# An attention, experts and delta-net stack: output products without waits in the merge, lower halves moved from GpSimd to VectorE, and fewer products in the stick-breaking sums

## Chip, cores and metric

One Trainium2 chip, one core of it. The metric is the device time of one execution in microseconds; lower is better. All data is float32. Products that must be exact to nearly 24 bits are made of three TensorE products of rounded halves (below).

## What is computed

The reference is two blocks on 512 tokens of width 1024. Only the parts that the change touches are shown.

```python
def rms_norm(x, g):                      # rmsnorm is the same
    return x * rsqrt(mean(x * x, -1) + EPS) * g

def first_block(x, ...):
    h = rms_norm(x, norm_attn)
    ...                                  # two attentions: o_mla, o_dil
    gates = sigmoid(gate_pre.reshape(B, S, 2, D) + b_gate)
    merged = gates[:, :, 0] * (o_mla @ w_o_mla) + gates[:, :, 1] * (o_dil @ w_o_dil)
    x = x + merged @ w_out               # the merge
    h2 = rms_norm(x, norm_ffn)
    return x + hier_moe(h2, ...)         # 32 experts, two for each token

def second_block(x, ...):                # layer 0: attention, layer 1: delta net
    for layer in range(2):
        h = rmsnorm(x, norm_mix_g[layer]) * (1.0 + scale_m) + shift_m
        x = x + gate_m * mixed(h)
        h = rmsnorm(x, norm_ffn_g[layer]) * (1.0 + scale_f) + shift_f
        x = x + gate_f * swiglu(h, ffn_w_in[layer], ffn_w_out[layer])
    return rmsnorm(x, final_norm_g)
```

Half of the heads of layer 0's attention are "stick" heads (stick-breaking attention): with z the scores and l = log(1 + exp(z)), the weight of key s for query t (s < t) is exp(z[s,t] - sum of l[r,t] over r from s to t-1). So each weight needs a sum of l over the keys from s on.

## The kernel before

Everything lies transposed: features or keys on the 128 partitions, the 512 tokens on the free axis. `xT` is the residual in 8 tiles of 128 x 512 (`KD` = 8). Five engines run programs of their own, in an order written out by hand, and meet at semaphores; `k.meet()` between stages makes every compute engine wait for the last work of the others.

**Split products.** A weight tile of 128 x 1024 (a unit) is loaded by DMA on SP's queue, its upper half is a rounded copy by ACT (`split_hi_act`, L338), its lower half is the difference, by DVE (`split_lo_dve`, L344) or by POOL (`split_lo_pool`, L353). `split_product_pe` (L463 to L465) then does, for each of 8 rows kk, three products of 512 columns: hi x hi, lo x hi, hi x lo. `low_mark` says which semaphore tells PE that a unit's lower half is there; `pool_units` is how many units POOL does. `load_weights_sp` loads a unit into one of four slots once the slot's former lower half has been taken. The ring of upper and lower halves has 3 places in the merge and 4 in the SwiGLU: `split_hi_act` for unit i waits for the product that is that many units back.

**Merge.** For j = 0 to 7 and both branches n, PE makes a gate product (a split product) and a plain product (L1562) into banks 4*(j%2) to 4*(j%2)+3. ACT takes the sigmoid, DVE multiplies (L1604, counted as `evacuated`), adds the two branches (L1607), makes lower halves of the units 2j+3 and 2j+4, and at last takes the lower half of the merged row j (L1611, counted as `merged`). Then follow 8 output products (units 16 to 23) into the banks 0 to 3: the first waits for `merged` 8, the ones for j = 1, 2, 3 wait for the addition of the product before (`added`, L1542), the later ones for the addition four products back.

**Norms.** While the last products run, ACT squares each row of x and POOL adds the squares up (`fold_pool`, L508); DVE makes the last addition (L515) and the stage ends in a meeting. Then PE sums over partitions (L519), ACT takes the root (L525; before it stands a load of ACT's table, ACT_TABLE_LOAD, since other functions were in use), DVE takes the reciprocal (L543), and for each of the 8 rows DVE multiplies (L550), ACT rounds (L535) and DVE takes the lower half (L559); PE's next products take the rows in turn. `norm` (before the experts and at the end) has no lower halves. `block_norm` (before layer 0's attention) and `split_norm` (before both SwiGLUs and the delta net) have weights converted beside them: two blocks by POOL, or unit 0 by DVE and units 1 to 3 by POOL. `first_norm` is another function.

**Stick.** For each of 8 heads, PE makes scores for key tiles j = 0 to 3 over the queries from j*128 on (512, 384, 256, 128 columns; L2505). DVE makes -|z| (L2576, L2578), ACT takes Exp and Ln (L2548, L2552; two table loads a head), DVE adds max(z, 0) and masks the first 128 columns (L2583, L2586), which gives l. For head h-1, PE then makes for each key tile i the score again (L2515), the mask (L2517), and minus the sums of l: `neg_from` times tile i's l and `neg_ones` times each later tile's (L2519, 4+3+2+1 products); ACT takes Exp (L2558) and copies into the same scratch. For head h-2, PE multiplies with the values (L2529) and DVE copies the result (L2590). All these products are float32 and show as two instructions each. The fourth tile of head h-1 goes into the bank that the first one had, so it waits for ACT's Exp of the first.

## Time and profile before

| what | value |
|---|---|
| median of 3 runs | 2894.82 us (2888.44 to 2900.26) |
| the profiled execution: its time, its span | 2895.99 us, 2894.7 us |
| busy share of the span: PE, DVE, ACT, POOL | 89%, 47%, 31%, 16% |
| mean granted TensorE clock | 0.934 of full |

Start times in rows of the trace count from the start of the span. The profiled execution ended 1.3 us after its span and was 1.2 us above the median of the runs. "Idle before" tells how long an engine stood still ahead of a group and what ended that.

### The profile page before, as it was taken

Reading aid. Unit: us, or ns where it says so; the run is one execution under the profiler, and the core shown is the slowest. Engines: PE = TensorE matmul, PEld = TensorE weight load, DVE = VectorE, ACT = ScalarE, POOL = GpSimd, SP = SyncE. Lnnn points to the kernel's source line nnn. Section 1 sums busy time; section 2 is a strip of 40 time slices with the busy share of each in tenths; the row PEclk is TensorE's granted clock in tenths of the full one; section 3 lists DMA queues with packets and bytes.
Section 4 is the critical chain, followed back from the end, with each engine's and each line's share of the span. In section 5 each row is a group of like instructions: output and inputs, shape, how many; then the busy total and the mean of one; then the engine's idle time right before and its main releaser. Section 6 shows DMA issues by size and latency. Waiting matters only on the chain.

```text
span 2894.7 us, 33686 instructions
## 1 busy us (share of the span) xinstructions
PE 2590.6 (89%) x13305; PEld 2049.3 (71%) x13305; DVE 1363.5 (47%) x2290; ACT 895.6 (31%) x1610; POOL 456.6 (16%) x449
## 2 busy tenths in 40 slices
PE   6999989998699994998988999979889899899997
PEld 4798987665455552876676878767787776687876
DVE  7886745322311114426537666345645644433333
ACT  4344435321211111325533212233322322332222
POOL 4563422000122222200011000010200200200001
PEclk9899988998799996998998999989989899899999
DMA  5453311132389994320014566232002002232322
GB/s 185 138 153 96 116 59 45 52 87 73 146 337 415 417 405 148 94 73 1 1 59 145 182 194 185 73 80 59 1 13 75 1 18 77 71 98 77 113 79 67
DMA packets 315084, 340.86 MB, mean 118 GB/s; under 512 B 18800, under 2 KB 271856, under 8 KB 302512
## 3 DMA queue, kind: packets, MB, share of 16 engines
q1 hardware_dynamic: 292720, 281.79, 29.7%
q0 software_dynamic: 22208, 56.93, 5.7%
q8 instruction: 106, 1.74, 0.3%
q14 instruction: 50, 0.41, 0.0%
HBM read 372.21 MB, written 16.78 MB: 134 GB/s over the span
## 4 chain that ended last, share of the span: by engine, by line
PE 72%; DVE 6%; ACT 4%; DMA 4%; issue 1%; ACTq 0%; POOL 0%; DVEq 0%; POOLq 0%
PE bank L463 13%; PE bank L465 13%; PE bank L464 13%; PE bank L2926 4%; PE bank L2166 4%; DMA sb_expert_weights<-w_up 3%; PE bank L2192 2%; PE bank L1562 2%; PE bank L399 2%; PE bank L401 2%; PE bank L400 2%; PE bank L669 1%; PE bank L689 1%; PE bank L679 1%; DVE sb_scratch L543 1%
## 5 line engine op out<-in xcount | busy, mean ns | idle before, releaser
L344 DVE TENSOR_TENSOR sb_w_lo<-sb_weights,sb_w_hi 128x1024 fp32r<-128x1024 f32 (+2 forms) x215 | 239.9, 1125 | 508.3 <-ACT sb_w_hi L338 508.0
L463 PE MATMUL bank<-sb_h_hi,sb_w_hi 128*128 128x512 f32 x1040 | 420.9, 405 | 7.1 <-DVE sb_w_lo L344 7.1
L465 PE MATMUL bank<-sb_h_hi,sb_w_lo 128*128 128x512 f32 x1040 | 408.3, 393 | 0.0
L464 PE MATMUL bank<-sb_h_lo,sb_w_hi 128*128 128x512 f32 x1040 | 407.7, 392 | 0.0
L338 ACT CAST sb_w_hi<-sb_weights 128x1024 fp32r<-128x1024 f32 x224 | 215.5, 969 | 555.2 <-PE bank L465 488.4
L508 POOL TENSOR_TENSOR sb_scratch<-sb_scratch 128x512 f32<-128x512 f32 x30 | 38.7, 1292 | 1309.3 <-ACT sb_scratch L498 1309.3
L463 PEld LDWEIGHTS bank<-sb_h_hi,sb_w_hi 128*128 128x128 f32 x1040 | 197.0, 189 | 61.6 <-issue 21.7
L464 PEld LDWEIGHTS bank<-sb_h_lo,sb_w_hi 128*128 128x128 f32 x1040 | 197.1, 189 | 45.7 <-issue 5.3
L399 PE MATMUL bank<-sb_wide,sb_h_hi 128*128 128x512 f32 (+2 forms) x512 | 206.4, 403 | 23.8 <-DVE sb_h_lo L556 8.6
L465 PEld LDWEIGHTS bank<-sb_h_hi,sb_w_lo 128*128 128x128 f32 x1040 | 196.4, 189 | 43.0
L400 PE MATMUL bank<-sb_wide,sb_h_hi 128*128 128x512 f32 (+2 forms) x512 | 199.2, 389 | 0.0
L401 PE MATMUL bank<-sb_wide,sb_h_lo 128*128 128x512 f32 (+2 forms) x512 | 199.0, 389 | 0.0
L463 PE MATMUL bank<-sb_hidden_hi,sb_w_hi 128*128 128x512 f32 x352 | 138.7, 394 | 12.9 <-DVE sb_hidden_lo L1772 12.9
L399 PEld LDWEIGHTS bank<-sb_wide,sb_h_hi 128*128 128x128 f32 x512 | 122.0, 238 | 37.8 <-issue 22.7
L465 PE MATMUL bank<-sb_hidden_hi,sb_w_lo 128*128 128x512 f32 x352 | 137.8, 391 | 0.0
L464 PE MATMUL bank<-sb_hidden_lo,sb_w_hi 128*128 128x512 f32 x352 | 137.7, 391 | 0.0
L381 DVE TENSOR_TENSOR sb_wide<-sb_weights,sb_wide 128x1024 fp32r<-128x1024 f32 (+2 forms) x62 | 88.2, 1427 | 98.3 <-ACT sb_wide L374 98.2
L2166 PE MATMUL bank<-sb_expert_weights,sb_moe 128*64 128x256 f32 x960 | 124.4, 385 | 9.4 <-DMA sb_expert_weights<-w_up 7.3
L401 PEld LDWEIGHTS bank<-sb_wide,sb_h_lo 128*128 128x128 f32 x512 | 122.1, 238 | 10.3
L400 PEld LDWEIGHTS bank<-sb_wide,sb_h_hi 128*128 128x128 f32 x512 | 122.6, 240 | 9.2
L374 ACT CAST sb_wide<-sb_weights 128x1024 fp32r<-128x1024 f32 (+2 forms) x72 | 72.0, 1003 | 167.7 <-PE bank L401 139.6
L2166 PEld LDWEIGHTS bank<-sb_expert_weights,sb_moe 128*64 128x64 f32 x960 | 77.7, 138 | 44.6 <-issue 13.6
(512 smaller groups left out, 4799.7 us busy)
## 6 DMA issues: line engine op xcount, KB each, us to landing
sb_weights<-ffn_w_in SPq DMA_DIRECT2D x88, 512.0 KB
sb_weights<-w_in SPq DMA_DIRECT2D x52, 512.0 KB
sb_xT<-ada_w POOLq DMA_DIRECT2D x24, 1024.0 KB, 6.8
sb_weights<-ada_w SPq DMA_DIRECT2D x24, 1024.0 KB
sb_expert_weights<-w_down SPq DMA_DIRECT2D x22, 1024.0 KB, 9.8
sb_expert_weights<-w_gate SPq DMA_DIRECT2D x20, 1024.0 KB, 12.6
sb_expert_weights<-w_up SPq DMA_DIRECT2D x19, 1024.0 KB, 15.2
sb_weights<-ffn_w_out SPq DMA_DIRECT2D x32, 512.0 KB
```

The costliest lines, as they stand in the source:

```text
L338: act.copy(u.hi[:, 0:u.kt, :], u.chunk.w).then_inc(*k.hi.one())
L344: dve.tensor_tensor(u.lo[:, 0:u.kt, :], u.chunk.w, u.hi[:, 0:u.kt, :].bitcast(F32), ALU.subtract).then_inc(*k.lo.one())
L374: act.copy(b.hi, b.chunk.w).then_inc(*k.block_hi.one())
L381: dve.tensor_tensor(b.lo, b.chunk.w, b.hi.bitcast(F32), ALU.subtract).then_inc(*k.block_lo.one())
L399: pe.matmul(out, hi[:, r, tokens], b.hi[:, kk, :], start=r == 0, stop=False)
L400: pe.matmul(out, hi[:, r, tokens], b.lo[:, kk, :], start=False, stop=False)
L401: return pe.matmul(out, lo[:, r, tokens], b.hi[:, kk, :], start=False, stop=last)
L463: pe.matmul(bank[:], u.hi[:, kk, :], act[0][:, kk, :], start=first and kk == 0, stop=False)
L464: pe.matmul(bank[:], u.hi[:, kk, :], act[1][:, kk, :], start=False, stop=False)
L465: mm = pe.matmul(bank[:], u.lo[:, kk, :], act[0][:, kk, :], start=False, stop=last and kk == u.kt - 1)
L2166: mm = pe.matmul(halves(bank, n)[:, 0:FF], r.xbT[p % 2][:, at:at + CAP], loads[n].w[:, kk, :], start=kk == 0, stop=kk == KD - 1)
L2926: mm = pe.matmul(bank[:, hh * P:(hh + 1) * P], left(hh), right(hh), start=True, stop=True)
```

## The change

The merge's first output product waits for the evacuation of the banks that it writes, and then row by row for the merged rows; the next three wait for no addition. In the norms ACT runs a Sqrt of one column into a new tile `early` before anything else. `block_norm`'s block 0 gets its lower half from DVE. `split_norm` leaves only unit 1 to POOL; DVE does unit 2 within the last rows of the norm and unit 3 after them. In the stick, the key tiles go in the order 3, 2, 1, 0; DVE adds the next tile's l into the tiles 2 and 1 (behind their first 128 columns, before the mask), so that PE needs only `neg_from` times tile i and one more product with tile i+1, whose matrix is `neg_before` or, for i = 0, `neg_ones`.

```diff
--- before.py
+++ after.py
@@ -79,7 +79,7 @@
         "chunk_all": chunk,
         "neg_from": -(part >= col).astype(np.float32),
         "neg_ones": -np.ones((P, P)),
-        "sb_keep": part < col,
+        "neg_before": -(part < col).astype(np.float32),
         "sb_mask": np.where(part < col, 0.0, NEG),
         "causal": np.where(col <= part, 0.0, NEG),
         "levels": np.concatenate(levels, 1),
@@ -519,6 +519,11 @@
     k.nc.tensor.matmul(k.bank[3][:], k.const("ones"), k.scr[10][:], start=True, stop=True).then_inc(*k.h_sum.one())
 
 
+def root_table_act(k):
+
+    k.nc.scalar.activation(k.early[:], k.eps[:], ACT.Sqrt).then_inc(*k.act_step.one())
+
+
 def norm_root_act(k, ready):
     act = k.nc.scalar
     act.wait_ge(*ready)
@@ -536,7 +541,7 @@
                            ).then_inc(*k.h_hi.one())
 
 
-def norm_rows_dve(k, gain, shift, split):
+def norm_rows_dve(k, gain, shift, split, late=None):
     dve = k.nc.vector
     inv = k.scr[4]
     dve.wait_ge(*k.h_root.at(1))
@@ -549,6 +554,8 @@
             h = k.scr[5 + kk % 4][:] if split else k.hT[:, kk, :]
             dve.scalar_tensor_tensor(out=h, in0=k.xT[:, kk, :], scalar=gain(kk), in1=inv[:], op0=ALU.mult,
                                      op1=ALU.mult).then_inc(*k.h_rows.one())
+        if late and kk == KD - 1:
+            split_lo_dve(k, late)
         if split and kk > 0:
             j = kk - 1
             dve.wait_ge(*k.h_hi.at(j + 1))
@@ -564,6 +571,7 @@
 def norm(k, gain):
 
     norm_sum_pe(k)
+    root_table_act(k)
     norm_root_act(k, k.h_sum.at(1))
     norm_rows_dve(k, gain, None, None)
 
@@ -571,8 +579,9 @@
 def block_norm(k, gain, shift, blocks):
 
     norm_sum_pe(k)
+    root_table_act(k)
     block_hi_act(k, blocks[0])
-    block_lo_pool(k, blocks[0])
+    block_lo_dve(k, blocks[0])
     norm_root_act(k, k.h_sum.at(1))
     block_hi_act(k, blocks[1])
     block_lo_pool(k, blocks[1])
@@ -582,16 +591,18 @@
 
 def split_norm(k, gain, shift, split, units):
 
-    k.pool_units = 3
+    k.pool_units = 1
     norm_sum_pe(k)
+    root_table_act(k)
     split_hi_act(k, units[0])
     norm_root_act(k, k.h_sum.at(1))
     for u in units[1:4]:
         split_hi_act(k, u)
-        split_lo_pool(k, u)
+    split_lo_pool(k, units[1])
     norm_shift_act(k, shift, split)
     split_lo_dve(k, units[0])
-    norm_rows_dve(k, gain, shift, split)
+    norm_rows_dve(k, gain, shift, split, units[2])
+    split_lo_dve(k, units[3])
 
 
 
@@ -944,7 +955,7 @@
     k.consts = k.sb("consts", [P, k.at_["dist0"][0]])
     k.rows = k.sb("rows", [P, sum(n for _, n in ROWS.values())])
     k.pos = k.sb("pos", [P, 2 * NT], I32)
-    k.eps, k.kgain = k.sb("eps", [P, 1]), k.sb("kgain", [P, 1])
+    k.eps, k.kgain, k.early = k.sb("eps", [P, 1]), k.sb("kgain", [P, 1]), k.sb("early", [P, 1])
     k.posf = k.sb("posf", [P, 2 * NT])
     k.cos1, k.sin1 = k.sb("cos1", [P, NT, ROPE // 2]), k.sb("sin1", [P, NT, ROPE // 2])
     k.cos2, k.sin2 = k.sb("cos2", [P, NT, ROPE2 // 2]), k.sb("sin2", [P, NT, ROPE2 // 2])
@@ -1563,11 +1574,11 @@
             mm.then_inc(*k.projected.one())
             ch.freed = [k.projected.last()]
     for j in range(KD):
-        if j < 4:
-            pe.wait_ge(*k.merged.at(KD) if j == 0 else k.added.at(j))
-        else:
+        if j == 0:
+            pe.wait_ge(*k.evacuated.at(2 * (KD - 1)))
+        elif j >= 4:
             pe.wait_ge(*k.added.at(j - 3))
-        split_product_pe(k, units[2 * KD + j], merged, k.bank[j % 4])
+        split_product_pe(k, units[2 * KD + j], merged, k.bank[j % 4], rows=None if j else k.merged)
 
 
 def merge_act(k, units, merged):
@@ -2490,6 +2501,9 @@
     pool.tensor_copy(padded[HD:P, 3:H:2, :], q[HD:P, 1:4, :]).then_inc(*k.padded_pool.one())
 
 
+STICK = (3, 2, 1, 0)
+
+
 def stick_pe(k, padded, kb, vb, o):
     pe = k.nc.tensor
     for s in range(H + 2):
@@ -2499,9 +2513,9 @@
             pe.wait_ge(*k.padded_act.at(h // 2 + 1))
             pe.wait_ge(*k.padded_dve.at(2))
         if h < H:
-            for j in range(NT):
+            for j in STICK:
                 if h >= 1:
-                    pe.wait_ge(*k.reduced.at(4 * (h - 1) + j + 1))
+                    pe.wait_ge(*k.reduced.at(4 * h - j))
                 pe.matmul(k.bank[j][:, 0:S - j * P], kb[:, h // 2, j * P:(j + 1) * P], padded[:, h, j * P:S],
                           start=True, stop=True).then_inc(*k.scored.one())
         h = s - 1
@@ -2515,9 +2529,11 @@
                 pe.matmul(bank[:, 0:n], kb[:, h // 2, i * P:(i + 1) * P], padded[:, h, i * P:S],
                           start=True, stop=False)
                 pe.matmul(bank[:, 0:P], k.const("ident"), k.const("sb_mask"), start=False, stop=False)
-                for j in range(i, NT):
-                    mm = pe.matmul(bank[:, (j - i) * P:n], k.const("neg_from" if j == i else "neg_ones"),
-                                   k.scr[4 * (h % 3) + j][:, 0:S - j * P], start=False, stop=j == NT - 1)
+                mm = pe.matmul(bank[:, 0:n], k.const("neg_from"), k.scr[4 * (h % 3) + i][:, 0:n], start=False,
+                               stop=i == NT - 1)
+                if i < NT - 1:
+                    mm = pe.matmul(bank[:, P:n], k.const("neg_before" if i else "neg_ones"),
+                                   k.scr[4 * (h % 3) + i + 1][:, 0:n - P], start=False, stop=True)
                 mm.then_inc(*k.turned.one())
         h = s - 2
         if 0 <= h < H:
@@ -2542,13 +2558,13 @@
     for s in range(H + 1):
         h = s
         if h < H:
-            for j in range(NT):
+            for j in STICK:
                 n, u = S - j * P, k.scr[4 * (h % 3) + j]
-                act.wait_ge(*k.maxed.at(4 * h + j + 1))
+                act.wait_ge(*k.maxed.at(4 * h + NT - j))
                 act.activation(u[:, 0:n], u[:, 0:n], ACT.Exp).then_inc(*k.exped.one())
-            for j in range(NT):
+            for j in STICK:
                 n, u = S - j * P, k.scr[4 * (h % 3) + j]
-                act.wait_ge(*k.exped.at(4 * h + j + 1))
+                act.wait_ge(*k.exped.at(4 * h + NT - j))
                 act.activation(u[:, 0:n], u[:, 0:n], ACT.Ln, bias=1.0).then_inc(*k.rooted.one())
         h = s - 1
         if h >= 0:
@@ -2568,22 +2584,27 @@
     for s in range(H + 2):
         h = s
         if h < H:
-            for j in range(NT):
+            for j in STICK:
                 n, u, z = S - j * P, k.scr[4 * (h % 3) + j], k.bank[j]
-                dve.wait_ge(*k.scored.at(4 * h + j + 1))
+                dve.wait_ge(*k.scored.at(4 * h + NT - j))
                 if h >= 3:
                     dve.wait_ge(*k.weighed.at(h - 2))
                 dve.tensor_scalar(u[:, 0:n], z[:, 0:n], 0.0, None, ALU.max).then_inc(*k.dve_step.one())
                 dve.wait_ge(*k.dve_step.last())
                 dve.scalar_tensor_tensor(out=u[:, 0:n], in0=u[:, 0:n], scalar=-2.0, in1=z[:, 0:n], op0=ALU.mult,
                                          op1=ALU.add).then_inc(*k.maxed.one())
-            for j in range(NT):
+            for j in STICK:
                 n, u, z = S - j * P, k.scr[4 * (h % 3) + j], k.bank[j]
-                dve.wait_ge(*k.rooted.at(4 * h + j + 1))
+                dve.wait_ge(*k.rooted.at(4 * h + NT - j))
                 dve.scalar_tensor_tensor(out=u[:, 0:n], in0=z[:, 0:n], scalar=0.0, in1=u[:, 0:n], op0=ALU.max,
                                          op1=ALU.add).then_inc(*k.dve_step.one())
                 dve.wait_ge(*k.dve_step.last())
-                dve.tensor_tensor(u[:, 0:P], u[:, 0:P], k.const("sb_keep"), ALU.mult).then_inc(*k.reduced.one())
+                if j in (1, 2):
+                    dve.wait_ge(*k.reduced.last())
+                    dve.tensor_tensor(u[:, P:n], u[:, P:n], k.scr[4 * (h % 3) + j + 1][:, 0:n - P], ALU.add
+                                      ).then_inc(*k.dve_step.one())
+                    dve.wait_ge(*k.dve_step.last())
+                dve.tensor_tensor(u[:, 0:P], u[:, 0:P], k.const("before"), ALU.mult).then_inc(*k.reduced.one())
         h = s - 2
         if 0 <= h < H:
             dve.wait_ge(*k.weighed.at(h + 1))
```

## Rows read from the trace of the kernel before

**Rows 1.** The page's chain that ended last: shares of the span by engine.
```profile
PE 72%; DVE 6%; ACT 4%; DMA 4%; issue 1%; ACTq 0%; POOL 0%; DVEq 0%; POOLq 0%
```

**Rows 2.** Waits of PE from 681 to 748 us: total, times, longest.
```profile
PE bank L463 <- DVE sb_xT L1542: 9.2, 3, 3.0
...
PE bank L463 <- DVE sb_merged_lo L1611: 4.5, 1, 4.5
```

**Rows 3.** Timeline of DVE at the end of the merge's gates: start, duration.
```profile
663.89 0.69 DVE L1604 TENSOR_TENSOR sb_scratch<-sb_scratch,bank 128x512 f32<-128x512 f32 x1 [8.21 <-PE bank L1562]
...
685.29 0.68 DVE L1611 TENSOR_TENSOR sb_merged_lo<-sb_scratch,sb_merged_hi 128x512 fp32r<-128x512 f32 x1
```

**Rows 4.** Windows of the merge: PE, PEld, DVE, ACT, POOL busy, clock, DMA, GB/s.
```profile
681.60:686.03 4.43, 0.00 (x0) 0.00 (x0) 4.25 (x5) 0.62 (x1) 0.00 (x0) 0.84 0.74 207
...
686.03:694.30 8.27, 8.22 (x24) 6.29 (x24) 0.00 (x0) 0.00 (x0) 0.00 (x0) 0.68 0.59 143
...
697.30:704.70 7.40, 7.37 (x24) 5.55 (x24) 0.00 (x0) 0.61 (x1) 0.00 (x0) 0.77 0.24 71
...
730.90:747.20 16.30, 16.30 (x73) 13.17 (x71) 3.21 (x4) 2.95 (x4) 3.87 (x3) 1.00 0.00 0
```

**Rows 5.** The last window before the experts' products.
```profile
780.00:803.00 23.00, 10.82 (x52) 10.05 (x52) 10.74 (x64) 0.20 (x1) 2.92 (x3) 0.50 0.09 24
```

**Rows 6.** Timeline of the norm before the first SwiGLU, all engines.
```profile
1523.78 1.04 ACT L338 CAST sb_w_hi<-sb_weights 128x1024 fp32r<-128x1024 f32 x1 [1.19 <-DVE sb_scratch L515]
...
1524.84 1.28 ACT L525 ACT_TABLE_LOAD   x1
...
1524.96 1.23 DVE L344 TENSOR_TENSOR sb_w_lo<-sb_weights,sb_w_hi 128x1024 fp32r<-128x1024 f32 x1 [1.64 <-ACT sb_w_hi L338]
...
1526.86 3.35 DVE L543 RECIPROCAL sb_scratch<-sb_scratch 128x512 f32<-128x512 f32 x1 [0.68 <-ACT sb_scratch L525]
...
1527.93 7.41 POOL L353 TENSOR_TENSOR sb_w_lo<-sb_weights,sb_w_hi 128x1024 fp32r<-128x1024 f32 x3 [9.40 <-ACT sb_w_hi L338]
...
1530.25 5.63 DVE L550 SCALAR_TENSOR_TENSOR sb_scratch<-sb_xT,sb_mod,sb_scratch 128x512 f32<-128x512 f32 x2
...
1536.59 0.80 PE L449 MATMUL bank<-sb_h_hi,sb_w_hi 128*128 128x512 f32 x1 [10.79 <-DVE sb_h_lo L559]
...
1543.76 1.62 DVE L559 SCALAR_TENSOR_TENSOR sb_h_lo<-sb_scratch,sb_mod,sb_h_hi 128x512 fp32r<-128x512 f32 x2
```

**Rows 7.** Instructions of line L550: minimum, median, maximum in ns.
```profile
L550 DVE SCALAR_TENSOR_TENSOR sb_scratch<-sb_xT,sb_mod,sb_scratch x32: 739/743/2881, 1156.5 to 2515.3; 128x512 f32<-128x512 f32 x32
```

**Rows 8.** Timeline of the norm before layer 0's attention.
```profile
1153.15 3.35 DVE L543 RECIPROCAL sb_scratch<-sb_scratch 128x512 f32<-128x512 f32 x1 [3.73 <-ACT sb_scratch L525]
...
1158.98 0.77 PE L399 MATMUL bank<-sb_wide,sb_h_hi 128*128 128x512 f32 x1 [6.68 <-DVE sb_h_lo L559]
```

**Rows 9.** Timeline of ACT: the table loads of the two plain norms.
```profile
752.17 1.28 ACT L525 ACT_TABLE_LOAD   x1 [3.55 <-PE bank L519]
...
2881.45 1.28 ACT L525 ACT_TABLE_LOAD   x1 [2.18 <-PE bank L519]
```

**Rows 10.** Window of the first pair of products after the SwiGLU's norm.
```profile
1541.10:1549.30 8.20, 8.20 (x37) 6.83 (x36) 4.15 (x7) 2.18 (x3) 0.00 (x0) 0.99 0.01 2
```

**Rows 11.** Window of one head of the stick.
```profile
1393.06:1406.12 13.06, 12.00 (x66) 9.09 (x65) 6.93 (x17) 7.51 (x15) 0.00 (x0) 1.00 0.01 1
```

**Rows 12.** Groups of the stick: count, busy us, mean ns, idle before.
```profile
L2515 PE MATMUL bank<-sb_arena 128*128 128x128 f32 x16 | 3.5, 302 | 6.4 <-ACT sb_scratch L2558 6.4
...
L2548 ACT ACTIVATE sb_scratch<-sb_scratch 128x512 f32<-128x512 f32 x8 | 5.0, 630 | 29.8 <-DVE sb_scratch L2578 29.8
```

**Rows 13.** Chain of the stick: start, duration, piece.
```profile
1368.35 2.16 PE bank L2519 x8
```

**Rows 14.** Windows that begin with a wait of PE, experts and delta net.
```profile
963.98:968.00 4.02, 1.95 (x19) 1.62 (x20) 0.00 (x0) 0.38 (x1) 0.30 (x1) 1.00 1.03 399
...
1989.21:1993.00 3.79, 1.75 (x6) 0.62 (x6) 1.64 (x4) 0.28 (x1) 0.00 (x0) 0.85 0.21 46
```

## The prediction, made before the changed kernel ran

> **What bounds the kernel now.** I read the chain that ended last first: TensorE (PE) holds 72% of it and DVE and ACT 10% together [rows 1]. So a saving counts where PE stands still or is made to do less on the chain, and nothing elsewhere. Then I took the three places that the change touches and read in each which wait of PE ends last.
>
> In the merge PE stands 4.5 us before the first output product, for the last merged row, and 3.0 us before each of the next three, for the addition of the product before [rows 2]. The windows show what else these waits cost: three undisturbed products take 16.30 us, 5.43 each, at clock 1.00, but the one after a wait takes 7.40 at a mean clock of 0.77 and the first 8.27 at 0.68 [rows 4]. A product behind a wait runs partly at the lower of the two levels.
>
> In the norm ahead of the first SwiGLU the reader sees DVE's first two row products take 5.63 us together [rows 6], where the median of such an instruction is 743 ns and the maximum 2881 [rows 7]. Beside them POOL makes three lower halves until 1535.3. PE waits for all of it until 1536.59 [rows 6]. The norm ahead of layer 0's attention has no POOL subtraction beside its row products: from the reciprocal's start to PE's it needs 5.83 us [rows 8], the other 9.73 [rows 6].
>
> In the stick one head takes 13.06 us, PE is busy for 12.00 of it [rows 11], and the piece that it waits for is ACT's: 6.4 us before the fourth tile of key scores, 1.06 in each of six heads [rows 12].
>
> **Merge.** The banks of the first four output products were evacuated at 664.6 [rows 3], so what they still wait for are lower halves of weights and the merged rows. PE ends the last plain product at 681.60 [rows 4] and goes straight on. Rows 1 to 7 of the first product are 21 instructions of 5.43/24 = 0.226, 4.75 us; row 8 is asked for at 686.35, and its lower half ends at 685.29 + 0.68 = 685.97 [rows 3]. That cover is thin, 0.4 us; without it the first product loses what is missing, no more. Unit 16 is split before, units 17 and 18 just ahead of row 8's lower half on DVE. Unit 19 is converted after the first product (687.0 + about 1.04 + 1.23 = 689.4, [rows 6] for the durations) and is due at 697.9. Its load and unit 20's leave SP's queue at 681.6, when the last plain weights are free, as before; the windows show 207 and 143 GB/s there [rows 4], at which 0.5 MB takes under 4 us. Additions, squares and POOL's sums then come one per 5.43 us as in the undisturbed products of before. Eight products take 43.5 us and end at 725.1 instead of 747.2: **-22.1 us**. What follows moves along: the experts' first weights are issued once the merge is over and are in long before PE takes them (DMA share 0.09 in the last 23 us ahead [rows 5]).
>
> **Table load.** It moves from between the first upper half and the root to the front. In the two plain norms ACT is idle for 3.55 and 2.18 us before it [rows 9]. The final addition and the meeting take 1.19 of that (the idle time before the upper half [rows 6]); 2.36 and 0.99 are left to hide the load of 1.28 and the one-column root. That root isn't in the trace; it lies between nothing and 0.69 (a root of 512 columns, from the gap between the load's end and the reciprocal [rows 6]), and I take 0.2, near the low end, as it has one column. So the first saves 1.28 and the last 0.99 - 0.2 = 0.8: **-2.1 us**. In the other four norms the load only changes places with an upper half, which comes 1.5 us later.
> The Trainium skill (ScalarE: Activation LUTs, What ACT_TABLE_LOAD costs) puts a drain of 1.38 us behind each load, 2.66 us for a switch. In the trace the reciprocal begins 0.74 us after the load's end, with the whole root between them [rows 6], so this case shows no drain there. By the page the plain norm ahead of the experts would gain some 0.9 us more, and the sum with it.
>
> **Three split norms.** Upper half 0 begins at 1523.8 + 1.28 + 0.2 = 1525.3 and ends at 1526.3; the root ends at 1527.0; DVE's lower half of 1.23 ends at 1527.7, and the reciprocal begins there, 0.85 later than before (1526.86). It ends at 1531.05. POOL has one subtraction left. It began 1.1 us after the root's end, so at 1528.1, and takes 7.41/3 = 2.47: it ends at 1530.6, before DVE's first row product [rows 6]. Why the reciprocal isn't stretched by POOL can be read off: it takes 3.35 with POOL at work beside it. PE then begins 5.83 us after the reciprocal's start [rows 8], at 1533.5 instead of 1536.6: -3.05 each, **-9.2 us** for three (the same lines stand ahead of the delta net and the second SwiGLU, and of the nine POOL subtractions six go).
> The two lower halves that move to DVE cost 1.15 to 1.23 each. Unit 2's stands before the lower halves of rows 7 and 8. The last of these ended at 1545.4 [rows 6]; PE reached row 8 six instructions before 1549.3, at 1548.0 [rows 10]. The slack of 2.6 takes in 1.2. Unit 3's comes after and is due a whole product after the pair. If the cover were gone, each would cost 1.2, 3.7 in all. Their slots come free some 10 us later, and SP waits there with the loads behind them; these units are due only after two more pairs, with the DMA idle (share 0.01 [rows 10]).
>
> **Block norm.** DVE now has a lower half of 1.23 between upper half 0 and the reciprocal, and it runs beside the root of 0.69: **+0.6 us** with the one-column root. POOL is freed sooner, and nobody waits for it.
>
> **Stick.** Per head three products go, of 256, 128 and 128 columns. 1280 columns take 2.16 us [rows 13], so 512 take 0.86. In six heads this lengthens the wait for ACT instead, from 1.06 to about 1.9. The loop that sets the head is scores, DVE, Exp, Ln, Exp (two table loads), fourth tile, values, scores. There the new order lets DVE start after 128 columns of scores instead of 512, 0.64 sooner, of which its copy of the head before leaves 0.45; but the last Exp is now 512 wide, 0.63 [rows 12], where it was 128 wide, about 0.3. Net -0.13, in six heads -0.8. In the first two heads DVE's longer reduction shows, about +0.5; in the last, which only PE bounds, -0.86, and some rounding: **-1.4 us**. DVE's additions (128 and 256 columns, together 0.7 to 0.8) are not on that loop, since the next tiles wait for scores first. The bounds: -0.86 in all eight heads, -7, if PE were the loop; +0.8 in all eight, +6, if DVE's additions came onto it.
>
> **Sum.** -22.1 - 2.1 - 9.2 + 0.6 - 1.4 = -34.2. The profiled execution took 2895.99, which gives 2861.8; it stood 1.2 above the median of the runs shown, a difference within their spread, and I leave it out. The likeliest case's own range is 2854 to 2869: the stick's bounds, and a few clock falls more or less at stalls that shift.
>
> **Rivals.**
> *The clock falls in the stick.* PE's wait grows from 1.06 to 1.9 us a head. After a 2.07 us wait in the experts the clock stays at 1.00, after a 2.04 us wait in the delta net it is 0.85 over wait and sequel [rows 14], so both happen. A fall costs 7.40 - 5.43 = 1.97 [rows 4]; six heads, 11.8: 2873.6.
> *POOL isn't the cause, or DVE's new load gives it back.* The margin of 0.4 between POOL's end and the first row product is small, and the late halves may hold PE up. For it speaks only that margin; against it the 5.83 us of the norm without POOL. The 9.2 are lost: 2871.0.
> *The merge keeps a stall.* If one of its four starts still waits, for unit 19 or row 8, 3.0 + 1.97 come back for each; two of them give 2871.7.
> *The gain isn't passed on.* The merge does what is said, but the experts wait for their weights: half of the 22 us is lost, 2872.9, all, 2883.9. The idle DMA ahead of them [rows 5] speaks against it.
> *Slower.* PE stays at the lower level through the stick: 12.00 - 0.86 = 11.1 us of a head's work become 22, some 9 more than the head has now. From four such heads on (35 us) the change loses; all eight give 2861.8 + 72 = 2934. Against it: 1.00 in every head today with 1.06 us of wait [rows 11].
>
> **How the numbers follow.** Forecast 0.68, clock in the stick 0.10, norms 0.08, a stall left in the merge 0.06, not passed on 0.05, slower 0.03. The range 2850 to 2877 holds the forecast with its bounds and the three rivals between 2871 and 2874. A difference under 0.5% (14.5 us, down to 2880.3) is about what a measurement of this kernel can't tell from none. Faster: all but the total loss of the merge's gain and the slower case, 0.92; within 0.5%: 0.05; slower: 0.03.
>
> **What would show it.** The merge: no wait of PE between the last plain product and the eighth output product, clock 1.00, 43.5 us. The norms: L550 at 743 ns throughout, PE 9.7 - 3.05 = 6.7 us after where the reciprocal began before; the table loads ahead of the column sum's end. The stick: heads of about 12.9 us with PE busy 11.1. Wrong would be: a stall behind row 8 or unit 19, lower clock after the longer waits of the stick, heads over 13.1 us, or row products that are still stretched.

## The result, and the profile after

The whole change takes 2866.16 us (median of 4 runs, 2862.68 to 2874.99); the kernel before, run beside it, 2891.63 (4 runs). The ratio is 0.9904 [0.9889, 0.9919]. By the medians that is -25.5 us, by the ratio -27.8; the forecast was -34.2 and 2862. The forecast's ratio would be 0.9882, just outside the interval: the time lies in the range that was given, but the gain is smaller than forecast by more than the noise. The profiled execution is the longest of the four: 2874.99 us, span 2873.7. Against before's profiled 2895.99 that is -21.0, so this trace shows 13 us less than the forecast, and the question is where they went.

The chain that ended last, shares of the span by engine, in the changed kernel:

```profile
PE 72%; DVE 6%; ACT 4%; DMA 4%; issue 1%; POOL 0%; ACTq 0%; DVEq 0%; POOLq 0%
```

It has the shares of before [rows 1]: the change took standing time out and left the bound where it was.

DVE in the merge of the changed kernel. L1615 is the last gate (L1604 before), L1622 the last merged row's lower half, L1553 the additions, L515 the norm's meeting:

```profile
682.58 0.69 DVE L1615 TENSOR_TENSOR sb_scratch<-sb_scratch,bank 128x512 f32<-128x512 f32 x1 [8.21 <-PE bank L1573]
...
686.19 0.68 DVE L1622 TENSOR_TENSOR sb_merged_lo<-sb_scratch,sb_merged_hi 128x512 fp32r<-128x512 f32 x1
...
690.26 0.68 DVE L1553 TENSOR_TENSOR sb_xT<-bank,sb_xT 128x512 f32<-128x512 f32 x1
695.71 0.68 DVE L1553 TENSOR_TENSOR sb_xT<-bank,sb_xT 128x512 f32<-128x512 f32 x1
...
726.07 0.69 DVE L1553 TENSOR_TENSOR sb_xT<-bank,sb_xT 128x512 f32<-128x512 f32 x1 [4.75 <-PE bank L465]
...
727.46 0.69 DVE L515 TENSOR_TENSOR sb_scratch<-sb_scratch 128x512 f32<-128x512 f32 x1 [0.70 <-ACT sb_scratch L498]
```

From L1615 to L515 are 44.88 us. The same way was 66.95 before, from 681.69 to 748.64: -22.07. The first additions follow each other by 5.45 us, as the undisturbed products of before did [rows 4], and the view of waits has none of PE from 660.5 to 728.

Windows of the changed kernel: the merge's end, a middle head of the stick, a head with a piece at the clock's lower level, and the end of the delta net (columns as in [rows 4]):

```profile
682.58:727.46 44.88, 43.45 (x192) 35.63 (x190) 15.46 (x19) 10.92 (x14) 7.74 (x6) 1.00 0.23 59
...
1405.82:1418.63 12.81, 11.14 (x60) 8.27 (x59) 7.55 (x20) 7.52 (x14) 0.00 (x0) 1.00 0.00 1
1369.78:1385.42 15.64, 13.96 (x58) 10.51 (x57) 7.92 (x19) 7.52 (x14) 0.00 (x0) 0.78 0.00 1
...
2336.70:2364.00 27.30, 23.87 (x92) 19.16 (x93) 7.33 (x18) 4.62 (x8) 0.00 (x0) 0.51 0.00 1
```

The merge has its eight output products, 192 instructions of PE, in 43.45 us at clock 1.00, which were eight times 5.43 in the forecast. Row 8 of the first was due at 687.11 and its lower half ended at 686.87: the thin cover was 0.24 us. An undisturbed head of the stick takes 12.81 (13.06 before, [rows 11]). But the head from 1369.78 on (counted from ACT's first Ln of one head to that of the next, so that the whole of one fall lies in it) takes 15.64 at a mean clock of 0.78, and 27 us at the delta net's end run at 0.51, the lower level (1.2 GHz) nearly throughout: eight products of line L3017 take 1.97 us there, where they took 1.06 before.

The norm ahead of the first SwiGLU, all engines, in the changed kernel (before: [rows 6]). L524 is the new root of one column, L530 the root, L548 the reciprocal, L555 the row product, L566 its lower half:

```profile
1503.82 1.28 ACT L524 ACT_TABLE_LOAD   x1 [1.19 <-DVE sb_scratch L515]
...
1505.11 0.20 ACT L524 ACTIVATE sb_early<-sb_eps 128x1 f32<-128x1 f32 x1
1505.22 1.03 ACT L338 CAST sb_w_hi<-sb_weights 128x1024 fp32r<-128x1024 f32 x1
1506.15 0.68 ACT L530 ACTIVATE sb_scratch<-bank,sb_eps 128x512 f32<-128x512 f32 x1
1506.38 1.23 DVE L344 TENSOR_TENSOR sb_w_lo<-sb_weights,sb_w_hi 128x1024 fp32r<-128x1024 f32 x1 [3.02 <-ACT sb_w_hi L338]
...
1507.52 3.35 DVE L548 RECIPROCAL sb_scratch<-sb_scratch 128x512 f32<-128x512 f32 x1
...
1507.93 2.38 POOL L353 TENSOR_TENSOR sb_w_lo<-sb_weights,sb_w_hi 128x1024 fp32r<-128x1024 f32 x1 [9.38 <-ACT sb_w_hi L338]
1510.90 1.41 DVE L555 SCALAR_TENSOR_TENSOR sb_scratch<-sb_xT,sb_mod,sb_scratch 128x512 f32<-128x512 f32 x2
...
1513.25 0.80 PE L449 MATMUL bank<-sb_h_hi,sb_w_hi 128*128 128x512 f32 x1 [7.64 <-DVE sb_h_lo L566]
...
1520.40 1.22 DVE L344 TENSOR_TENSOR sb_w_lo<-sb_weights,sb_w_hi 128x1024 fp32r<-128x1024 f32 x1
```

POOL ends at 1510.31, 0.59 before DVE's first row product, and the first two row products take 1.41 us, where it was 5.63. All 32 of them, minimum, median, maximum in ns, where the maximum was 2881 [rows 7]:

```profile
L555 DVE SCALAR_TENSOR_TENSOR sb_scratch<-sb_xT,sb_mod,sb_scratch x32: 743/747/752, 1132.4 to 2492.7; 128x512 f32<-128x512 f32 x32
```

From L515 to PE's first product it is 10.59 us; before it was 13.96 (1522.63 to 1536.59). ACT and PE in the norm ahead of the experts of the changed kernel, then PE in the norm ahead of layer 0's attention:

```profile
728.61 1.28 ACT L524 ACT_TABLE_LOAD   x1 [1.19 <-DVE sb_scratch L515]
729.90 0.20 ACT L524 ACTIVATE sb_early<-sb_eps 128x1 f32<-128x1 f32 x1
730.07 0.69 ACT L530 ACTIVATE sb_scratch<-bank,sb_eps 128x512 f32<-128x512 f32 x1
```
```profile
1125.48 2.04 PE L519 MATMUL bank<-sb_scratch,sb_consts 128*128 128x512 f32 x2 [5.91 <-DVE sb_scratch L2304]
...
1134.80 0.76 PE L399 MATMUL bank<-sb_wide,sb_h_hi 128*128 128x512 f32 x1 [7.27 <-DVE sb_h_lo L566]
```

**Stage by stage, profiled execution against profiled execution.** Up to the merge's last gate +0.9. Merge -22.1. Norm ahead of the experts, from the meeting to the reciprocal, 5.64 to 3.42: -2.2. Norm ahead of the attention, from the column sum to PE, 8.73 to 9.32: +0.6. Three split norms 3.37 each (one of them 14.67 to 11.31): -10.1. Last norm -1.2. Together the edits outside the stick give -35.0. Against that stand the stick, 112.45 us from its first score to the start of its last evacuation before and 117.33 after (+4.9), and stages that nobody edited: the delta net from PE's first product to the next norm's meeting 560.4 and 567.3 (+6.9), the last SwiGLU +2.8, the rest -1.5.

The first SwiGLU, in that rest, deserves a look of its own: 383.2 us before, 383.8 after. In the four traces with the norms of before it took 382.8 to 383.2 us, in the ten with changed norms, experiments included, 383.6 to 384.8. All have the same wait of 3.1 us some 326 us in (PE for DVE's lower half of the hidden rows); the 10 us from the start of that wait show a mean clock of 1.00 before (1860.40 to 1870.40) and 0.83 in the changed kernel (1836.30 to 1846.30), and the clock falls there in each of the ten and in none of the four. So the changed norms lose 0.4 to 2.0 us again in the stage behind them. Why the same wait brings a fall there isn't shown.

### The profile page after: what moved, and what is told of

It is laid out like the page before. It is cut to its first block, busy times and chain, and to the rows that moved or that the text cites. A ratio compares the mean times of both kernels' runs of the same rounds, so it can differ in the third digit from the quotient of the medians.

```text
span 2873.7 us, 33625 instructions
## 1 busy us (share of the span) xinstructions
PE 2591.9 (90%) x13257; PEld 2050.9 (71%) x13257; DVE 1363.8 (47%) x2313; ACT 894.8 (31%) x1616; POOL 437.1 (15%) x442
## 4 chain that ended last, share of the span: by engine, by line
PE 72%; DVE 6%; ACT 4%; DMA 4%; issue 1%; POOL 0%; ACTq 0%; DVEq 0%; POOLq 0%
PE bank L463 13%; PE bank L464 13%; PE bank L465 13%; PE bank L2947 5%; PE bank L2177 4%; PE bank L2203 2%; PE bank L1573 2%; PE bank L399 2%; PE bank L400 2%; PE bank L401 2%; PE bank L680 1%; DMA sb_expert_weights<-w_up 1%; DMA sb_weights<-w_up 1%; PE bank L700 1%; PE bank L3030 1%
## 5 line engine op out<-in xcount | busy, mean ns | idle before, releaser
L344 DVE TENSOR_TENSOR sb_w_lo<-sb_weights,sb_w_hi 128x1024 fp32r<-128x1024 f32 (+2 forms) x221 | 247.2, 1127 | 487.5 <-ACT sb_w_hi L338 487.3
```

What stands on the lines that cost most here:

```text
L344: dve.tensor_tensor(u.lo[:, 0:u.kt, :], u.chunk.w, u.hi[:, 0:u.kt, :].bitcast(F32), ALU.subtract).then_inc(*k.lo.one())
```

## The experiments

Every time is a median. Ratios, with their 95% intervals in brackets, are to the kernel before, run on the same chip. Its medians: 2895.81 us beside e1 to e4, 2895.64 beside e5, e6, e7 and e11, 2893.55 beside e10, e12 and e14, 2897.89 beside e15.

**e1_merge_only.** Before, with the changed `merge_pe` alone:

```diff
-        if j < 4:
-            pe.wait_ge(*k.merged.at(KD) if j == 0 else k.added.at(j))
-        else:
+        if j == 0:
+            pe.wait_ge(*k.evacuated.at(2 * (KD - 1)))
+        elif j >= 4:
             pe.wait_ge(*k.added.at(j - 3))
-        split_product_pe(k, units[2 * KD + j], merged, k.bank[j % 4])
+        split_product_pe(k, units[2 * KD + j], merged, k.bank[j % 4], rows=None if j else k.merged)
```

> The kernel before with the merge's waits alone changed. If the sum's first term is right and passed on, the merge's last eight products take 43.5 us instead of 65.6 and the whole kernel is 22 us faster (ratio 0.9924). If part of the gain is lost downstream (a later stage that waits for weights or stands at the lower clock because it begins elsewhere), the merge still shows 22 in its own windows and the total shows less, by the 8 us that are missing in the whole change: about -14. If the missing part belongs to the norms or the stick, -22.

2872.72 us, 0.9914 [0.9899, 0.9928], -23 to -25 us: what the merge shows in its own windows arrives in the whole time.

**e2_norms_only.** Before, with the changed `norm_rows_dve`, `norm`, `block_norm` and `split_norm`:

```diff
-    k.pool_units = 3
+    k.pool_units = 1
     norm_sum_pe(k)
+    root_table_act(k)
...
-    norm_rows_dve(k, gain, shift, split)
+    norm_rows_dve(k, gain, shift, split, units[2])
+    split_lo_dve(k, units[3])
```

> The kernel before with the norms alone changed (early root of one column, lower halves moved). By the prediction's terms -2.1 for the two plain norms, three times -3.05, +0.6 for the block norm: -10.7 us (ratio 0.9963). If the norms are where the sum fell short, -2 to -5.

2884.23 us, 0.9953 [0.9937, 0.9969]: -11.6 by the medians, -13.6 by the ratio, as expected within the interval.

**e3_stick_only.** Before, with the changed `stick_pe`, `stick_act` and `stick_dve` and their matrix:

```diff
-            for j in range(NT):
+            for j in STICK:
...
-                for j in range(i, NT):
-                    mm = pe.matmul(bank[:, (j - i) * P:n], k.const("neg_from" if j == i else "neg_ones"),
+                mm = pe.matmul(bank[:, 0:n], k.const("neg_from"), k.scr[4 * (h % 3) + i][:, 0:n], start=False,
...
```

> The kernel before with the stick alone changed. If the stick's own structure decides, heads of 12.8 us instead of 13.07 in the middle, a start about 1 us longer, and -1 to -2 us in all. If the longer waits of PE in it make TensorE's clock fall, one or more heads of over 15 us as in the changed kernel's trace, and +3 to +6 us in all. If the falls come from where the work happens to lie and not from the waits, the stick here has as many of them as in the kernel before (none in its middle).

2897.55 us, 1.0007 [0.9997, 1.0017]: +2.0 [-0.9, +4.9]. One head in its trace, and PE's wait for ACT, 1.67 us, ahead of the fourth tile:

```profile
1411.42:1425.26 13.84, 12.17 (x60) 9.30 (x60) 7.55 (x19) 7.53 (x14) 0.00 (x0) 0.92 0.00 1
```
```profile
1408.50 0.46 PE L2518 MATMUL bank<-sb_arena 128*128 128x128 f32 x2 [1.67 <-ACT sb_scratch L2563]
```

The wait has grown from 1.06 [rows 12] to 1.67, and the clock falls within one middle head, while before has it at 1.00 in all of them.

**e4_no_stick.** The whole change, with the three functions of the stick as before (e3's diff the other way round).

> The whole change without the stick's part. If the stick costs 3 to 6 us by clock falls, this is that much faster than the whole change: about -30 to -33 us against the kernel before (ratio 0.989). If the stick is a gain or neutral, it equals the whole change or is 1 to 2 us slower, about -24 to -27.

2858.54 us, 0.9863 [0.9843, 0.9884]: it beats the whole change, and by more than was expected (-37 us by the medians). So the stick's part loses time inside the whole.

**e5_after_again.** The whole change once more, no edit.

> The whole change once more, unedited, so that it stands in one comparison with the three that follow. The whole change was 0.9904 [0.9889, 0.9919] of before, merge and norms without the stick's part 0.9863 [0.9843, 0.9884]. If the stick's part really costs some 8 us inside the whole, this is again at 0.989 to 0.992 (about 2866 us); if the difference between those two measurements was chance, it falls to 0.987 to 0.988 (about 2859 us). In the trace: the stick's scores to its last product about 126 us, with some 20 to 30 us of it at the lower clock level.

2866.82 us, 0.9909 [0.9891, 0.9927]: the first measurement stands. Its trace differs: span 2861.4, 12.3 under the other's. The stick takes 113.69 there, 117.8 to PE's last product, where about 126 was expected, with one middle head at a mean clock of 0.92:

```profile
1388.38:1402.19 13.81, 12.13 (x60) 9.27 (x60) 7.55 (x19) 7.53 (x14) 0.00 (x0) 0.92 0.00 1
```

and the delta net 558.5, where it was 567.3 in the first trace of the same kernel.

**e15_no_stick_again.** e4 once more, no edit.

> Merge and norms without the stick's part, once more and unedited. Its first measurement had four runs, 0.9863 [0.9843, 0.9884]; the whole change was 0.9904 and, repeated, 0.9909. The forecast's own terms without the stick's give -32.8 us, 0.9887; read from the traces, merge and norms are worth 35.0 us, 0.9879. If the stick's part costs what its stage shows in the traces (1.2 to 4.9 us), this comes out at 0.987 to 0.990. If it costs the 12 us that the first ratios differ by, it comes out at 0.986 again.

2862.01 us, 0.9873 [0.9852, 0.9895]. It lies between the two answers. With e4's runs the version without the stick's part is at about 0.987, the whole change with e5's at 0.991: by the kernels' own medians the stick's part costs 4 to 8 us, by the ratios about 11 (0.9907 - 0.9869), with an uncertainty of some 6. Its delta net took 567.4, e4's 560.3.

**e6_stick_filler.** The whole change, with one overwritten product ahead of each head's second scores, 0.86 us of PE:

```diff
+                if i == 0:
+                    pe.matmul(bank[:, 0:n], kb[:, h // 2, i * P:(i + 1) * P], padded[:, h, i * P:S],
+                              start=True, stop=True)
                 pe.matmul(bank[:, 0:n], kb[:, h // 2, i * P:(i + 1) * P], padded[:, h, i * P:S],
```

> Ahead of each head's first product of the second score, the same product runs once more and is overwritten (0.86 us of TensorE, eight times); nothing else differs from the whole change. TensorE's wait ahead of the fourth tile, 1.67 us in the whole change and 1.06 before, shrinks to about 0.8. Theory A, the stretches at the lower clock come from the longer waits: a head takes 12.8 us as now, the lower-level stretches shrink to before's 13.7 us, and the time is 4 to 8 us under the whole change (2858 to 2862 us). Theory B, where those stretches fall has nothing to do with these waits: the same as the whole change within 3 us (2863 to 2869). Theory C, TensorE sets the head's time: 0.86 x 8, some 7 us slower (2873).

2868.04 us, 0.99 [0.9883, 0.9918]. A middle head of it:

```profile
1374.25:1387.06 12.81, 11.99 (x62) 8.65 (x62) 7.56 (x19) 7.53 (x14) 0.00 (x0) 1.00 0.00 0
```

The trace agrees with theory A: 0.86 us more work, the same 12.81, a wait of 0.8, and no middle head under clock 1.00. The time agrees with theory B: nothing is won over e5. In its trace the delta net took 567.4 us, in e5's 558.5, which is more than the stick could win. That filling the wait wins the time back is not shown.

**e7_order_only.** The whole change, with the ten sum products of before and no additions on DVE; the order 3, 2, 1, 0 stays:

```diff
...
-                if j in (1, 2):
-                    dve.wait_ge(*k.reduced.last())
-                    dve.tensor_tensor(u[:, P:n], u[:, P:n], k.scr[4 * (h % 3) + j + 1][:, 0:n - P], ALU.add
-                                      ).then_inc(*k.dve_step.one())
```

> Merge and norms as in the whole change; of the stick's part only the order of a head's tiles, 3 first, while the sums are ten products for four tiles again and VectorE adds nothing up. TensorE's work per head is back at about 12.0 us, the wait ahead of the fourth tile at about 0.8 to 1.1. Theory A (the waits bring the lower level): heads of about 12.8 to 12.9 us and few at the lower level, 2857 to 2861 us. Theory B: whatever TensorE has to do, the order alone leaves the time where the whole change has it, 2864 to 2869. If the head's time is set by the work of TensorE and not by the round through ScalarE: like the stick before, 13.06 a head, 2859.

2861.89 us, 0.9886 [0.9868, 0.9904], 4.9 under e5 by the medians, with overlapping intervals; it lies between the two theories and decides neither. A middle head, and its wait:

```profile
1374.96:1387.77 12.81, 12.01 (x66) 9.10 (x66) 6.84 (x17) 7.53 (x14) 0.00 (x0) 1.00 0.00 0
```
```profile
1384.85 0.46 PE L2529 MATMUL bank<-sb_arena 128*128 128x128 f32 x2 [0.80 <-ACT sb_scratch L2572]
```

With 12.01 us of work on PE a head takes the same 12.81 as with 11.14. All that a middle head gained came from the order; the removed products only lengthened the wait.

**e11_fourth_place.** The whole change, and a bank for the fourth tile. The scores of tiles 2 and 3 share bank 2, so bank 3 is free:

```diff
+def score_place(k, j):
+    return k.bank[j][:, 0:S - j * P] if j < 3 else k.bank[2][:, 2 * P:3 * P]
...
-                bank = k.bank[4 + m % 3]
-                if m >= 3:
-                    pe.wait_ge(*k.act_copied.at(m - 2))
+                bank = k.bank[(4, 5, 6, 3)[i]]
+                if h >= 1:
+                    pe.wait_ge(*k.act_copied.at(m - 3))
...
-                dve.wait_ge(*k.scored.at(4 * h + NT - j))
+                dve.wait_ge(*k.scored.at(4 * h + NT - min(j, 2)))
```

> The whole change, and the second score's fourth tile gets a PSUM bank of its own, so that it waits for no exponential of the same head: scores of tiles 2 and 3 share one bank (VectorE starts a head when both are there, some 0.3 us later), and the bank that this frees holds the fourth tile. Theory A' (the head's time of 12.81 us is the round through that wait, and TensorE's own 11.14 us lie under it): the 1.67 us wait goes, a head takes 11.2 to 11.6 us, 1.2 to 1.6 less eight times, 10 to 13 us, and if the waits also bring the lower level, 5 us more: 2848 to 2856 us. Rival (the round through VectorE and ScalarE, 9.87 us from a head's first maximum to its last mask, with the later start and the table loads, is as long as now): a wait of the same size appears at the scores, 2864 to 2870 us.

2854.53 us, 0.9861 [0.9841, 0.988]: 12.3 under e5, measured beside the same runs of before. PE in a head of it, then the head's window:

```profile
1378.48 0.39 PE L2533 MATMUL bank<-sb_arena 128*128 128x128 f32 x2
...
1379.15 2.34 PE L2549 MATMUL bank<-sb_arena,sb_scratch 128*128 128x64 f32 x20
```
```profile
1370.42:1381.33 10.91, 10.91 (x61) 8.21 (x60) 7.65 (x19) 7.43 (x15) 0.00 (x0) 1.00 0.00 0
```

The fourth tile's product waits for nothing, and PE is busy from end to end: 10.91 us a head, less than the 11.2 to 11.6 expected.

**e14_fourth_ten.** e7 with e11's edit: ten sum products and the fourth bank.

> The tile order alone with ten sum products (a head took 12.81 us, TensorE's own work 12.0) and the fourth tile's own bank beside it. With that bank and the seven-product sums a head took 10.90 us, with no wait left on TensorE. Theory: the round through ScalarE hid what the removed products are worth, and with that round gone they are worth their 0.86 us and the cheaper queue: a head takes 11.75 to 12.1 us here, 7 to 9 us slower than the version with seven, 2861 to 2864 us. Rival: the fourth bank alone brings all of it and another round sets 10.9 us: 2853 to 2856 us.

2856.63 us, 0.9885 [0.9868, 0.9902]. A head:

```profile
1370.85:1382.63 11.78, 11.78 (x67) 9.03 (x66) 6.92 (x17) 7.42 (x14) 0.00 (x0) 1.00 0.00 0
```

11.78 against 10.91, both with no wait. In the length of a head the three removed products are worth 0.87 us as soon as the fourth tile no longer waits, and nothing before that. The head came out as the theory said; the whole time, 2856.63, lies below the theory's 2861 to 2864 and just above the rival's 2856. The times of whole kernels don't resolve this step: e14's ratio is that of e7 although its heads are 1.03 us shorter, and e11's interval overlaps e14's.

**e10_first_only.** e1, but the products of tiles 1 to 3 wait for their additions as before:

```diff
-        elif j >= 4:
-            pe.wait_ge(*k.added.at(j - 3))
+        else:
+            pe.wait_ge(*k.added.at(j if j < 4 else j - 3))
```

> Before, with merge's output products of plain tile 0 alone waiting for no addition: those of tiles 1 to 3 still wait for the addition into their tile (they are issued after it was ordered, though). By the forecast's own terms tile 0's share is the 4.45 us wait ahead of it and the 2.9 us that the clock's lower level adds to its products, about 7 us of the 22.1, and the other three are 5.02 us each, 15 us: 2888 us, 0.9975 of before, and the way from the last plain gate to the last addition 59 to 60 us in place of 66.95. Rival: the waits are a chain of which the first alone sets the rest, and all of the 22 us go with it: 2873 us, 0.992.

2886.44 us, 0.9975 [0.9962, 0.9988]. DVE from the last gate to the norm's meeting:

```profile
679.30 0.69 DVE L1604 TENSOR_TENSOR sb_scratch<-sb_scratch,bank 128x512 f32<-128x512 f32 x1 [8.21 <-PE bank L1562]
...
739.04 0.69 DVE L515 TENSOR_TENSOR sb_scratch<-sb_scratch 128x512 f32<-128x512 f32 x1 [0.69 <-ACT sb_scratch L498]
```

59.74 us: tile 0's share of the 22.07 is 7.21, the other three have 14.86, 4.95 each.

**e12_tuned_fourth.** e11, with less done in the norms:

```diff
@@ block_norm @@
-    root_table_act(k)
     block_hi_act(k, blocks[0])
-    block_lo_dve(k, blocks[0])
+    block_lo_pool(k, blocks[0])
@@ split_norm @@
-    root_table_act(k)
```

> The version with the fourth tile's own bank (0.9861 [0.9841, 0.988] of before), with the norms trimmed: the block norm as before the change (lower half on the pool engine, no table load ahead), and no table load ahead in the three split norms, whose late lower halves stay on VectorE. By the forecast's terms the block norm gives 0.6 us back; in the split norms the early load hid nothing, since the rescaling activation behind it ended the wait: the root starts 0.2 us sooner without the small activation. Expected: 1 to 2 us under that version, 2852 to 2854 us, within 0.5% of it. Rival: the early load does pay there, 1.28 us each, and this is 3 to 4 us slower than it, 2858 us.

2845.15 us, 0.982 [0.9793, 0.9846], the best of all: by the medians 48 us under the kernel before. The norm ahead of the first SwiGLU:

```profile
1488.54 1.28 ACT L530 ACT_TABLE_LOAD   x1
1488.66 1.23 DVE L344 TENSOR_TENSOR sb_w_lo<-sb_weights,sb_w_hi 128x1024 fp32r<-128x1024 f32 x1 [1.64 <-ACT sb_w_hi L338]
...
1490.56 3.35 DVE L548 RECIPROCAL sb_scratch<-sb_scratch 128x512 f32<-128x512 f32 x1 [0.67 <-ACT sb_scratch L530]
...
1496.29 0.80 PE L449 MATMUL bank<-sb_h_hi,sb_w_hi 128*128 128x512 f32 x1 [7.10 <-DVE sb_h_lo L566]
```

From L515 (1486.33) to PE are 9.96 us, where the whole change has 10.59 and before 13.96: the lower half now lies beside the table load and hinders nothing. The block norm takes 8.79 from its column sum to PE (9.32, before 8.73). That makes some 4 x 0.6 = 2.4 us. The median is 9.4 under e11's, where 1 to 2 us were expected; the intervals overlap, e12's profiled span (2843.8) is even above e11's (2840.9), and the norms explain 2.4 of the 9.4. The rest is not shown to come from the edit.

## Why the prediction was right, and where it was off

**Merge: right in mechanism and size.** -22.1 forecast, -22.07 in the trace, no wait of PE, clock 1.00 (0.68 to 0.84 in the windows of [rows 4]). The thin cover ahead of row 8 held with 0.24 us, where 0.4 was forecast. e10 divides it as the terms had it: 4.45 + 2.9 = 7.3 for the first stall (7.21), 3 x 5.02 for the others (4.95 each). e1 shows that it is passed on, -23 to -25 us.

**Plain norms: right, the size low.** -2.1 forecast, -3.4 measured (-2.2 and -1.2). The one-column root took the 0.20 that I had taken. Of the first norm's surplus the missing piece is in e1, which has no early load and still needs only 4.90 from the meeting to the reciprocal, 0.74 less than before. Before, the clock has fallen ahead of PE's column sum (clock 0.50 from 750.02 to 752.07), and its two instructions take 2.05 us; in the changed kernel it is still at 1.00 from 728.83 to 729.68, and they take 1.20. The four traces in which the products of tiles 1 to 3 wait for an addition have 2.04 to 2.05 there, the ten others 1.20 to 1.54. The last norm gave 1.2 instead of 0.8 because the meeting is shorter there: ACT's load comes 0.90 us after its last work, and I had carried over the 1.19 of another norm. The Trainium skill (ScalarE: Activation LUTs, What ACT_TABLE_LOAD costs) puts a drain of 1.38 us behind a load; the trace has the load's end at 729.89 and the next activation at 729.90, so this case doesn't show it.

**Split norms: right.** -3.05 forecast, -3.37 measured, three times. POOL's subtraction took 2.38 instead of the 2.47 taken, and the moved lower halves (1520.40 here) brought PE no wait. What the step priced but didn't question was the early table load there: it delays the first lower half and so the reciprocal by 0.63 (e12), since ACT has other work to do in front of the root. What it left out is the stage behind: in the first SwiGLU 0.4 to 2.0 us are lost again (above).

**Block norm: right,** +0.6 forecast, +0.59 in the first trace and +0.43 in e5's.

**Stick: the mechanism right, the term mis-sized; the rival in part.** The loop that was named (scores, DVE, Exp, Ln, Exp, fourth tile, values, scores) is the one that sets the head. e7 shows it from one side (12.81 at either amount of work), e11 from the other (10.91 with the wait gone). Its parts as written add up to -0.8 + 0.5 - 0.86 = -1.2; no row gives the 0.2 of "rounding" that make it -1.4. A head was to lose 0.13 and lost 0.27, the wait was to grow to 1.9 and grew to 1.67. Without its one fall, e5's trace comes out close to the forecast, at -1.5, partly by luck: five head-to-head distances of 12.81 instead of 13.08 give -1.3 to -1.4, the start +0.5, the end -0.6. But every undisturbed middle head was counted at clock 1.00. In the three traces with the 1.67 us wait the clock fell in at least one middle head. In the eleven others, with waits of 1.06, 0.8 or none, it fell in none. In e5 one fall costs 2.7 us over two heads. The stick's term measured +1.1 in e3, +1.2 in e5 and +4.9 in the first trace, instead of -1.4. In the first trace two falls stand behind such waits, one in the middle heads and one behind the last (a mean clock of 0.78 from 1427.46 to 1443.20), and its start has a mean clock of 0.65, where before has 0.75. The rival had this mechanism but six falls, 11.8 us; it was one or two. That the wait brings the fall is argued from 3 traces against 11 and e6's clean heads; a trace is one execution, e6's time didn't follow, and the same long wait in a SwiGLU brought a fall in some traces and none in others.

**The sum.** -34.2 was forecast. What the traces give for the edits is -35.0 and +1.2 to +4.9, -30 to -34. The measured -25 to -29 is less, and the gap is in no edited stage; 0.4 to 2.0 us of it are in the first SwiGLU, behind the changed norms. The first trace has 6.9 us more in the delta net and 2.8 in the last SwiGLU; e5's has -1.9 and +2.9 there and, with a span 33.3 under before's, nearly the forecast. Two runs of one kernel differ here by as much (e4 and e15: 560.3 and 567.4). So that part is the spread of executions. That the whole came within 5 us of the forecast owes something to the norms, which gave 2.2 us more in the first trace than their terms and so hid a part of the stick's miss. Merge and norms add up: e1 and e2 together give -35 to -39, the version with both (e4, e15) -36 to -40. With e3's +2.0 the whole should be at -33 to -37, and it is at -25 to -29. Why the version without the stick's part is ahead by 4 to 11 us, when its stage shows 1.1 to 4.9, stays open: whether the stick's end shifts the falls in the stages behind it couldn't be told apart from that spread.

## What to carry to other kernels

Work taken off an engine is worth nothing while a round through other engines sets the loop. Look for the buffer that closes that round: here one more PSUM bank for the fourth tile made the head 1.9 us shorter, 0.87 of it the three removed products, which had been worth nothing in the length of a head. A stall costs its length and, when the clock falls, a piece of what follows (here 5.0 us for a wait of 3.0), so removing stalls can pay more than their sum and lengthening one may cost more than its growth. Measure a stage in several executions before you explain a few us of it, and look at the stages behind an edit too. Load a table early where ACT has nothing else to do before the root (the two plain norms, 1.1 to 1.5 and 1.2 us gained); where other work of ACT stands in front of the root, the load delays what the next engine waits for (0.63 us in a split norm).

## What the runs showed of the hardware

The granted clock varied between executions of one program: over the delta net it was 0.91 in the first trace of the whole change and 0.93 in e5's. In that stage, whose products no version edits, the way from the first product of line L449 to the next norm's meeting took 557.8 to 560.5 us in nine traces and 563.7 to 567.4 in the other five, and two kernels (the whole change, and the one without the stick's part) are in both groups. The last SwiGLU took 370.5 to 370.6 in five traces and 372.1 to 373.5 in nine. A wait of 3.1 us of PE in the first SwiGLU left the clock at 1.00 in four traces and brought a fall in ten. A POOL subtraction of two inputs beside DVE's row products stretched these from 0.74 to 2.88 us, yet DVE's reciprocal took 3.35 us beside POOL and alone.
